# Expert down weights stored as neighbouring rows, gate and up weights read as every second or third column

## The reference, cut to what matters

```python
def swiglu(h, w_gate, w_up, w_down):
    return (jax.nn.silu(h @ w_gate) * (h @ w_up)) @ w_down

def moe_swiglu(h, router_w, w_gate, w_up, w_down):
    ...
    top_vals, top_idx = lax.top_k(logits, TOP_K)
    top_w = jax.nn.softmax(top_vals, axis=-1)
    combine = jnp.sum(jax.nn.one_hot(top_idx, N_EXPERTS, dtype=jnp.float32) * top_w[..., None], axis=1)
    out = jnp.zeros_like(tokens)
    for e in range(N_EXPERTS):
        y = swiglu(tokens, w_gate[e], w_up[e], w_down[e])
        out = out + combine[:, e:e + 1].astype(tokens.dtype) * y
```

## Time and profile before

| what | value |
|---|---|
| median of three runs | 2075.43 us (2072.21 to 2075.69) |
| profiled execution | 2068.59 us, span 2066.5 us |
| expert stage, from the routing's end to the last instruction | from about 1200 to 2066.5 us |
| TensorE busy / weight loads busy | 1962.6 us (95%) / 1738.4 us (84%) |
| VectorE / ScalarE / GpSimd busy | 405.0 / 272.6 / 88.0 us |
| TensorE's granted clock, mean | 0.984 of full speed |
| bytes moved by DMA | 482.90 MB, 214758 packets |

### The profile page before, as it was taken

One profiled execution on the slowest core, in us unless ns is written; L12 is line 12 of the kernel. 1 busy time (PEld: TensorE's weight loads), 2 busy tenths in 40 slices (PEclk: granted clock), 3 DMA queues, 4 the chain that ended last, 5 costly groups with the idle time before them and its releaser, 6 DMA issues.

```text
span 2066.5 us, 66358 instructions
## 1 busy us (share of the span) xinstructions
PE 1962.6 (95%) x31022; PEld 1738.4 (84%) x31022; DVE 405.0 (20%) x900; ACT 272.6 (13%) x580; POOL 88.0 (4%) x174
## 2 busy tenths in 40 slices
PE   7999999999999999999999889999999999999997
PEld 6887787887777688787788779999989898989897
DVE  3335331111000133533311210000010101010001
ACT  1213213100000112222220100000000000000001
POOL 4010101000000001011000000000000000000000
PEclk9999999999999999999999899999999999999999
DMA  7413123456443142221335479999999999999996
GB/s 237 123 42 103 43 65 102 160 192 216 163 142 102 41 144 63 82 63 43 102 122 189 168 284 407 407 407 407 407 407 407 407 407 407 407 407 407 407 407 247
DMA packets 214758, 482.90 MB, mean 234 GB/s; under 512 B 11582, under 2 KB 110092, under 8 KB 214668
## 3 DMA queue, kind: packets, MB, share of 16 engines
q1 hardware_dynamic: 214668, 481.54, 62.6%
HBM read 480.46 MB, written 1.05 MB: 233 GB/s over the span
## 4 chain that ended last, share of the span: by engine, by line
PE 84%; DMA 6%; SPq 4%; DVE 4%; issue 1%; ACT 1%; POOL 0%; DVEq 0%
PE bank L1122 29%; PE bank L619 20%; PE bank L1091 7%; DMA pool<-in_moe_w_down_dram 6%; PE bank L680 5%; PE bank L1038 4%; PE bank L1071 4%; SPq L2050 3%; PE bank L1053 3%; PE bank L644 2%; PE bank L1231 1%; SPq L2055 1%; PE bank L672 1%; PE bank L1001 1%; DVE pool L1753 0%
## 5 line engine op out<-in xcount | busy, mean ns | idle before, releaser
L1122 PE MATMUL bank<-pool 128*64 128x80 f32 x21504 | 758.3, 234 | 31.5 <-DMA pool<-in_moe_w_down_dram 23.1
L1122 PEld LDWEIGHTS bank<-pool 128*64 128x64 f32 x21504 | 752.3, 138 | 38.8 <-DMA pool<-in_moe_w_down_dram 25.2
L619 PE MATMUL bank<-hnT,pool 128*128 128x256 f32 x1984 | 458.3, 386 | 1.6 <-DVE hnT L1573 1.6
L619 PEld LDWEIGHTS bank<-hnT,pool 128*128 128x128 f32 x1984 | 373.6, 192 | 61.2 <-issue 7.8
L1091 PEld LDWEIGHTS bank<-hnT,pool 128*128 128x128 f32 x704 | 134.9, 192 | 28.3 <-issue 10.8
L1091 PE MATMUL bank<-hnT,pool 128*128 128x256 f32 x704 | 157.1, 382 | 1.0 <-issue 1.0
L1958 DVE TENSOR_TENSOR pool<-pool,bank 128x320 f32<-128x320 f32 x32 | 15.6, 488 | 635.9 <-ACT pool L1526 635.9
L680 PEld LDWEIGHTS bank<-pool 64*64 64x64 f32 x3008 | 95.6, 135 | 18.3 <-issue 11.4
L680 PE MATMUL bank<-pool 64*64 64x64 f32 (+1 forms) x3008 | 105.2, 221 | 4.6 <-DVE pool L1599 3.6
L1526 ACT ACTIVATE pool<-bank 128x320 f32<-128x320 f32 x32 | 14.0, 437 | 673.5 <-PE bank L1122 673.5
L557 POOL TENSOR_TENSOR pool<-pool,level_mask 128x256 f32<-128x256 f32 x72 | 51.9, 735 | 796.4 <-DVE pool L1675 511.0
(11 more groups left out here) (322 smaller groups left out, 1196.3 us busy)
## 6 DMA issues: line engine op xcount, KB each, us to landing
pool<-in_moe_w_up_dram SPq DMA_DIRECT2D x128, 896.0 KB, 16.6
pool<-in_moe_w_gate_dram SPq DMA_DIRECT2D x128, 896.0 KB, 16.5
pool<-in_w_in_dram SPq DMA_DIRECT2D x66, 1024.0 KB, 5.3
pool<-in_moe_w_down_dram SPq DMA_DIRECT2D x64, 1024.0 KB, 16.6
pool<-in_moe_w_down_dram SPq DMA_DIRECT2D x32, 1536.0 KB, 18.6
pool<-in_ffn_w_gate_dram SPq DMA_DIRECT2D x11, 1024.0 KB, 7.7
pool<-in_ffn_w_up_dram SPq DMA_DIRECT2D x11, 1024.0 KB, 6.3
pool<-in_ffn_w_down_dram SPq DMA_DIRECT2D x11, 1024.0 KB, 5.1
```

Of the source, the lines that this page charges most:

```text
L619: ins = mm(ps[:, s * T:(s + 1) * T], w[:, k, (j + s) * P:(j + s + 1) * P], hnT[:, k, :], start=(k == 0), stop=(k == KD - 1))
L1122: ins = mm(bank[rows, cs], w[:, rows], rhs, start=start, stop=stop, skip_group_check=True)
```

## The change

A partition of a down buffer now holds two neighbouring rows of w_down (three in the last buffer): partition p of buffer 0 has rows 2p and 2p + 1. In high-speed memory these are 8 KB (12 KB) in one piece, and so they are in the partition. Tile f of the buffer is then every second (third) row. To keep hidden features and rows in the same order, hidden tile f takes every second column of the 256 that belong to its buffer (tiles 0 to 3), or every third of 384 (tiles 4 to 6). The gate and up weights are loaded as before; the matmul reads them with a step of 2 or 3 columns. The number of transfers, of matmuls and of bytes stays the same, and so do all waits.

```diff
@@ slot_tiles, in the hidden part of a round
                             for k in range(2):
                                 for f in groups[g]:
+                                    d = min(f // 2, 2)
+                                    lo, size = 2 * d * P, (3 if d == 2 else 2) * P
+                                    cols = slice(lo + f - 2 * d, lo + size, size // P)
                                     at = f - groups[g][0]
                                     ins = columns_mm(hidden_banks[g][s], slice(at * CAP, (at + 1) * CAP),
-                                                     hidden_slot(n)[:, k, f * P:(f + 1) * P], xgT[:, 2 * kk + k, :],
+                                                     hidden_slot(n)[:, k, cols], xgT[:, 2 * kk + k, :],
                                                      start=(kk == 0 and k == 0 and at == 0),
                                                      stop=(kk == KH - 1 and k == 1))
@@ down_load
-                src = a["moe_w_down"][0, e, rows, :].rearrange("a (f p) n -> p (a f) n", p=P)
+                src = a["moe_w_down"][0, e, rows, :].rearrange("a (p f) n -> p (a f) n", p=P)
                 sp_.dma_start(down_slot(n), src).then_inc(dwn_loaded[n], 16)
```

## The result

The changed kernel takes 2094.31 us (median of four, 2090.82 to 2096.86) against 2075.56 us of the kernel before (median of four): a ratio of 1.0101, 95% interval 1.0083 to 1.0119. It is slower by 18.8 us. The forecast was 2065.6 us and faster; the measured time lies outside the range and on the other side.

What follows compares the result with a forecast made beforehand. Transfers at 407 GB/s were taken to bound the expert stage; from the median of 2075.4 us, -9.8 us for joined packets and nothing for strided weights or the rest gave 2065.6 us, range 2055 to 2081.

Steps and rivals of the forecast that it cites:

- What bounds the kernel: Expert stage: transfers at 407 GB/s set the 108.2 us pass; TensorE needs 103.1 to 104.8 and waits 27.8 us.
- Part 1, the packets: Down loads: joined rows make 512 fewer packets a round at 9.9 ns fixed price each, -9.8 us over 31 rounds.
- Rival A: Down loads: packets stay at 4 KB, so nothing changes, 2075.4 us; chance 0.13.
- Rival B: Down loads: packets join but save less, 2.6 us, giving 2072.8 us; chance 0.10.
- Part 2: Expert stage: the transfer gain reaches the end, as TensorE still waits 2 to 4 us a pass; cap 27.8 us.
- Part 3, the strided weights: Gate and up weight loads with steps of 2 and 3 stay hidden: taken as 0, bounds 0 and about +290 us.
- Rival C: Weight loads with a step of 3 take 85 ns and set the pace: about 2095 us; chance 0.16.
- The deciding point: Rival C's threshold in the expert stage: above about 10 ns more a pair (30 us), TensorE's waits are used up.

Runs made afterwards that it cites:

- the packets alone: Kernel before with the change's long-packet down loads, gate and up tiles read as neighbouring columns: 2063.13 us, ratio 0.9952.
- 24 and 16 packets fewer on each engine a round: Against the kernel before: three row pairs and a single plain tile 6, 2065.47 us; pairs in down buffers 0 and 1 alone, 2068.48 us.
- the step of 4: Kernel before with hidden tiles 0 to 3 reading every fourth of 512 weight columns, transfers as before: 2233.26 us, one run.
- steps alone: Kernel before with steps of 2 and 3 in the gate and up weight loads, down rows loaded as before: 2093.84 us, ratio 1.0106.

## Why the prediction was wrong

*What bounds the kernel* held. Transfers at 407 GB/s set the pass, TensorE had 27.8 us of waits to give, and the single tile with a step of 3 showed those waits being spent.

*Part 1, the packets*, held: -9.8 us expected, -9.4 measured for the packets alone; that the two are so close is luck, with an interval 7 us wide. Firmer is the length of a pass, 1.29 us less where 4 x 0.317 = 1.27 was expected. 24 and 16 packets fewer on each engine a round gave -7.1 and -4.1 us where -7.1 (with the added transfer) and -4.9 were expected. Rival A is refuted by the packet count. Rival B (-2.6 us) is refuted by the time, and with it the estimate of -3.6 us from the Trainium skill's page DMA: Bandwidth & Descriptors, section "Why small descriptors are slow (HBM only)": joining packets paid far above its 256 bytes here, where the queue is the limit.

*Part 2* held for the packets alone: of TensorE's 3.4 to 5.1 us of slack in a pass, the faster transfers took 1.29 us (108.18 - 106.89), and it named the cap. It held only as long as TensorE's work stayed the same.

*Part 3, the strided weights, is the step that failed.* It priced a load with a step at 0 because a plain load hides. That reason says how much slack there is, 69.6 ns for a load of about 57, and nothing about what a step does to the load. The measured term is 96 x 32 = 3072 pairs at 19.4 ns, 59.6 us; less the 27.8 us of waits it leaves 31.8 us. The two profiled spans differ by 28.2 us (2094.7 - 2066.5), and the medians by 18.8.

The 28.2 us are made up as follows. 5.7 us lie ahead of the expert stage, whose first matmuls start at 1193.30 us before and at 1198.98 us after; the change does nothing there, and runs differ there without it (1193.0 us with the step of 4, 1196.1 with steps alone). In the stage the difference is 22.5 us. The first pass, which had no wait for a transfer to give, is 7.6 us longer, the full price of 7.46. The other seven are 15.0 us longer together, where 7 x 7.46 - 27.8 = 24.4 would be expected. The missing 9.4 us are what the waits of before cost beyond their own length. One part is the clock: two stretches of 224 matmuls took 9.61 us in place of 7.97, 3.3 us for both. (Other such stretches, behind waits as long, took 7.97.) Each came behind a wait of 2.13 us, and the first 3.46 us of one show the lower level, 1.2 GHz (length, busy times of PE and PEld, then clock, DMA share, GB/s):

```profile
1609.04:1612.50 3.46, 3.46 (x52) 3.46 (x54) 0.51 1.02 408
```

With no waits left, the granted clock of the changed kernel is 1.00, the upper level of 2.4 GHz, in every window from 1210 to 2085 us. The other part is the stopping itself: the 592 + 80 + 224 matmuls of a pass in the earlier trace rows take 31.98 us in three pieces, where 34.8 ns each makes 31.2. That is 0.8 us in each of five passes, and some 2 us more are lost in the other two, together about 6 us. So the waits could take up some 37 us of a slower TensorE, and not 27.8.

From the spans to the medians the rest is the choice of executions: the profiled one of before was 7.0 us below its median, the one of after 2.6 us above. Steps alone, in another batch, came out 21.3 us above the kernel before.

*Rival C was what happened*, with 0.16 of the chance. It guessed 85 ns a pair, the middle between two rows; it is 89. Its time of 2095 us against the measured 2094.3 is partly luck: 20 us remained in its sum, where 31.8 do by the measured price, and the 9.4 us that the waits gave back beyond their length were in neither. The deciding point, about 10 ns a pair, was passed by nearly twice.

*What should have been weighed otherwise*: the rows gave a factor of 1.22 before harm, and the rule of the Trainium skill's page Advanced Engine Details and Errata, section "SBUF Cachelines", put a step of 3 on the wrong side of it. A term with bounds of 0 and +290 us and a margin this thin, on an engine whose waits were 27.8 of 826 us, could have been the largest in the sum and got its most favourable value.

## What to carry to other kernels

When a transfer layout is bought with a strided read, price the read before the transfer: count the 16-byte pieces that one load touches, multiply by the price measured here (1.87 ns), and compare with the time that the matmul gives the load to hide in. Here pairs of float32 rows in a partition kept the loads hidden and gained 7 us, and three rows in the last buffer turned the gain into a loss of 19. And where two resources are both nearly full, a gain on one can't be kept once the other has become the limit, so the two halves of such a change have to be timed apart.

## What the runs showed of the hardware

A pair of loads of 64 float32 weight columns each took about 61 ns with a step of 2, 89 with 3, 120 with 4 and 118 with 7; with neighbouring columns it is 57 by estimate. A packet of the hardware queue cost about 9.9 ns plus 0.0366 ns a byte; fitted at 1 and 3.5 KB, this gave the gain of joined rows of 8 and 12 KB within the noise (-9.4 us measured for -9.8, a pass 1.29 us shorter for 1.27). What was not tried: steps in the streamed operand, and a step with weights of two bytes.
